# A two-block network on one core: the down product of both FFNs, from four blocks of K to one pass of eleven K pairs

## The reference, cut to what matters

```
def swiglu(x, w_gate, w_up, w_down):
    return (jax.nn.silu(x @ w_gate) * (x @ w_up)) @ w_down
f1 = swiglu(rms_norm(x, ffn1_pre_g), ...)
x = x + 0.5 * rms_norm(f1, ffn1_post_g)
m = token_mixer(rms_norm(x, mix_pre_g), ...)
x = x + rms_norm(m, mix_post_g)
f2 = swiglu(rms_norm(x, ffn2_pre_g), ...)
x = x + 0.5 * rms_norm(f2, ffn2_post_g)
```

## Time and profile before

| | us |
|---|---|
| median of 3 timed runs | 4001.05 |
| lowest and highest of them | 3992.30, 4002.52 |
| the profiled execution itself | 3995.18 |
| its span in the profile | 3993.3 |
| first down phase, 481.83 to 742.31 | 260.48 |
| second down phase, 1990.30 to 2251.30 | 261.00 |

### The profile page before, as it was taken

How to read it: one execution, slowest core, us unless ns; L and a number is a source line. 1 busy time by engine, 2 the same in 40 slices (tenths; PEclk the granted TensorE clock), 3 DMA queues, 4 the chain that set the end, 5 groups by cost and what they waited for, 6 DMA issues and landing times.

```text
span 3993.3 us, 50138 instructions
## 1 busy us (share of the span) xinstructions
PE 3769.9 (94%) x19892; PEld 3051.9 (76%) x19892; DVE 2422.4 (61%) x3232; ACT 1640.2 (41%) x2775; POOL 1788.9 (45%) x1176
## 2 busy tenths in 40 slices
PE   6999998899999899899989899999999999999998
PEld 4788776566665466788777689999968988888877
DVE  6655588744455538666578786654477436666664
ACT  4333333422222234333333443421283346666663
POOL 1555577344544452455577334332261233344364
PEclk9999999999999899999999999999999999999989
DMA  2222331110000021222331001121112310000024
GB/s 102 79 85 85 130 108 53 53 44 26 23 22 16 16 101 57 76 82 80 121 129 53 16 32 50 41 102 64 51 54 70 118 48 29 22 29 29 24 67 139
DMA packets 102218, 252.28 MB, mean 63 GB/s; under 512 B 12321, under 2 KB 15937, under 8 KB 101601
## 3 DMA queue, kind: packets, MB, share of 16 engines
q1 hardware_dynamic: 90096, 204.71, 15.2%
q0 software_dynamic: 9328, 41.75, 2.8%
q10 hardware_dynamic: 2560, 2.61, 0.2%
HBM read 200.47 MB, written 48.56 MB: 62 GB/s over the span
## 4 chain that ended last, share of the span: by engine, by line
PE 69%; DVE 17%; POOL 5%; ACT 5%; issue 3%; DMA 1%; SPq 0%; ACTq 0%; DVEq 0%; POOLq 0%
PE ps L936 6%; PE ps L937 6%; PE ps L938 6%; PE ps L418 5%; PE ps L419 5%; PE ps L420 5%; PE ps L4143 4%; PE ps L4075 2%; PE ps L4077 2%; PE ps L4076 2%; PE ps L1886 2%; PE ps L1888 2%; PE ps L1887 2%; PE ps L4127 2%; POOL fwl L820 2%
## 5 line engine op out<-in xcount | busy, mean ns | idle before, releaser
L392 POOL TENSOR_TENSOR wlo<-raw,whi 128x1024 fp32r<-128x1024 f32 x154 | 377.0, 2452 | 472.2 <-ACT whi L383 472.2
L418 PE MATMUL ps<-xh,whi 128*128 128x352 f32 (+1 forms) x1400 | 473.4, 338 | 6.1 <-DVE xl L674 2.7
L419 PE MATMUL ps<-xh,wlo 128*128 128x352 f32 (+1 forms) x1400 | 450.6, 322 | 0.0
L420 PE MATMUL ps<-xl,whi 128*128 128x352 f32 (+1 forms) x1400 | 450.0, 321 | 0.0
L820 POOL TENSOR_TENSOR fwl<-fpa,fwh 128x512 fp32r<-128x512 f32 x184 | 261.4, 1432 | 285.4 <-ACT fwh L811 283.2
L820 POOL TENSOR_TENSOR fwl<-fpb,fwh 128x512 fp32r<-128x512 f32 x180 | 258.1, 1444 | 291.1 <-ACT fwh L811 288.9
L4448 POOL TENSOR_TENSOR ospl<-osp,osph 128x672 fp32r<-128x672 f32 (+4 forms) x144 | 191.0, 1327 | 357.9 <-ACT osph L4269 356.8
L954 PE MATMUL ps<-fxh,fwh 128*128 128x512 f32 x616 | 255.5, 415 | 60.5 <-DVE acc L1167 30.3
L418 PEld LDWEIGHTS ps<-xh,whi 128*128 128x128 f32 x1400 | 265.1, 189 | 17.6 <-issue 5.7
L419 PEld LDWEIGHTS ps<-xh,wlo 128*128 128x128 f32 x1400 | 264.6, 189 | 8.0 <-issue 2.2
L1122 DVE TENSOR_TENSOR u<-ps,u 128x512 f32<-128x512 f32 x120 | 82.6, 689 | 301.0 <-PE ps L938 301.0
(11 more groups left out here) (506 smaller groups left out, 10113.7 us busy)
## 6 DMA issues: line engine op xcount, KB each, us to landing
raw<-in_w_dram SPq DMA_DIRECT2D x154, 512.0 KB, 3.7
fpa<-in_fg_dram SPq DMA_DIRECT2D x88, 256.0 KB, 3.6
fpb<-in_fg_dram SPq DMA_DIRECT2D x88, 256.0 KB, 3.4
hs_scratch<-u SPq DMA_DIRECT2D x88, 256.0 KB, 2.0
fyh<-hs_scratch SPq DMA_DIRECT2D x46, 256.0 KB, 5.9
fyl<-hs_scratch SPq DMA_DIRECT2D x42, 256.0 KB, 5.3
rs_scratch<-res POOLq DMA_DIRECT2D x2, 4160.0 KB, 14.3
frc<-in_fd_dram SPq DMA_DIRECT2D x32, 256.0 KB, 5.7
```

The source lines that it names most:

```text
L392: pool.x.tensor_tensor(K.wlo[n % 3][:, :], K.raw[n % 2][:, :], K.whi[n % 3][:, :], ALU.subtract).then_inc(*S.up("w_lo", n))
L418: pe.x.matmul(out, wh, xh, start=k == 0, stop=False)
L419: pe.x.matmul(out, wl, xh, start=False, stop=False)
L420: last = pe.x.matmul(out, wh, xl, start=False, stop=k == K - 1)
```

## The change

The blocks are gone. Each product runs over all eleven pairs before the next begins (steps ("down", m, k)), so each product is added up in PSUM and read once: 28 totals for an FFN. The bank sets are (0, 1, 2, 6) and (7, 4, 5, 3), and the order M1, M5, M6, M3, M7, M2, M4 alternates between them throughout. Sums change engines: DVE makes the weight sums (`dve_down_sum`), POOL makes the row sums, and only for M6, M7 and M4 (`pool_row_sum`). The row sum of M5 is no longer made in the down phase: the gate phase stores a third tile D for each j, the difference of its two halves (22 more stores, with one DVE subtraction each). Weights and rows stream through rings of eight tiles; D tiles of the first eleven j are kept in SBUF (`ftop`), running sums of weights in `fsum`. There are 88 weight loads and 88 row loads for an FFN. SP waits, load by load, for the user of the ring place eight loads before.

The mixed rows at the start of an FFN are split anew: POOL does 4 subtractions for M5 and 8 for M4, ACT 12 scalings, DVE 28 instructions; ACT's high parts of M4's rows, ahead of the gate steps before, now stand in the second of them, still ahead of the read of M1. Behind the first FFN, norm a (half 0, complete after M7) is squared, summed, rooted and partly applied inside the steps of M4; behind the second FFN all of the norms' work stands behind the last step, the sums of squares too.

```
-            if n == NSTEP - 1:
-                after.beside(p)
         S.steps[f, n] = "pe_step", (f, n)
+        if m == "M4":
+            after.beside(k)
...
+def dve_down_sum(dve, f, n):
+    if not FIRST_DOWN <= n < NSTEP or STEPS[n][1] not in RAW_SUMS:
+        return
+    _, m, k = STEPS[n]
+    total, at = K.fsum[k], RAW_AT[n]
+    for i in at:
+        slot_landed(dve, f, i)
+    first = raw_slot(K, at[0])
+    if m == "M5":
+        dve.wait_ge("pe_step", (f, STEP_AT["gate", 21, "M4"]))
+        out, x, y, op = total, first, raw_slot(K, at[1]), ALU.add
+    elif m == "M6":
+        dve.wait_ge("fw_lo", (f, STEP_AT["down", "M5", k]))
+        out, x, y, op = total, total, first, ALU.subtract
+    else:
+        dve.wait_ge("dve_fsum", (f, STEP_AT["down", "M6", k]))
+        out, x, y, op = first, first, total, ALU.subtract
+    dve.x.tensor_tensor(out, x, y, op).then_inc(*S.up("dve_fsum", (f, n)))
...
+def pool_row_sum(pool, f, n):
+    if not FIRST_DOWN <= n < NSTEP or STEPS[n][1] not in ("M6", "M7", "M4"):
+        return
+    at, top = ROW_AT[n], K.ftop[k]
+    for i in at:
+        row_landed(pool, f, i)
+    first = row_slot(K, at[0])
+    if m == "M7":
+        x, y = first, row_slot(K, at[1])
     else:
+        pool.wait_ge(f"ld_ft{k % 4}", (f, k))
+        x, y = (first, top) if m == "M6" else (top, first)
+    pool.x.tensor_tensor(first, x, y, ALU.subtract).then_inc(*S.up("ft_sum", (f, n)))
...
+A_BANKS, D_BANKS = (0, 1, 2, 6), (7, 4, 5, 3)
+def down_bank(m, p):
+    return (A_BANKS if m in ("M1", "M6", "M7", "M4") else D_BANKS)[p]
...
     for n in range(FIRST_GATE, NSTEP):
         pool_operand(pool, f, n + 4)
-        if FIRST_DOWN <= n + 5 < NSTEP:
-            raw_sum(pool, f, n + 5)
+        pool_row_sum(pool, f, n + 5)
...
         dve_row_low(dve, f, n + 3)
-        dve_row_sum(dve, f, n + 4)
+        dve_down_sum(dve, f, n + 5)
+        if STEPS[n][1] == "M4":
+            after.beside(STEPS[n][2])
...
+        for i, q in zip(RAW_AT[n], DOWN_RAWS[m]):
+            if i >= 8:
+                user = RAW_USER[i - 8]
+                sp.wait_ge("dve_fsum" if STEPS[user][1] in ("M5", "M6") else "fw_lo", (f, user))
+            sp.x.dma_start(raw_slot(K, i), A["fd"][f - 1, int(q), k])
...
+        for i, (c, past) in zip(ROW_AT[n], DOWN_ROWS[m]):
+            if i >= 8:
+                user = ROW_USER[i - 8]
+                if i - 8 == ROW_AT[user][0]:
+                    sp.wait_ge("ft_lo", (f, user))
+                else:
+                    sp.wait_ge("ft_sum", (f, user))
```

More of the change, by code:

```diff
@@ L460, in __init__ @@
         self.second, self.pairs = second, pairs
-        self.head = tag in ("n1", "n3")
+        self.head = not second
         if second:
@@ L713, in _ffn_steps @@
         out.extend(("gate", j, m) for m in ORDER)
-    for b, (k0, k1) in enumerate(BLOCKS):
-        for m in ORDER:
-            out.extend(("down", b, m, k) for k in range(k1 - k0))
+    for m in ORDER:
+        out.extend(("down", m, k) for k in range(KT))
     return out
@@ L751, in raw_landed, with slot_landed, row_landed @@
 def raw_landed(e, f, step, q):
[L753 to L766, removed]
+    e.wait_ge(f"ld_fr{step[1] % 2}{q}", (f, "gate", step[1], 0))
+def slot_landed(e, f, i):
+    e.wait_ge(f"ld_fr{i // 4 % 2}{i % 4}", (f, "down", i))
+def row_landed(e, f, i):
+    e.wait_ge(f"ld_fh{i % 8}", (f, i))
 def same(step, m):
-    return STEP_AT[step[:2] + (m,) + step[3:]]
+    return STEP_AT[step[:2] + (m,)]
 def raw_sum(e, f, n):
     S, K, step = e.S, e.K, STEPS[n]
-    if step[0] == "std" or step[2] not in RAW_SUMS:
+    if step[0] != "gate" or step[2] not in RAW_SUMS:
         return
@@ L806, in act_operand @@
         act.wait_ge(*S.unit_free(last - (last - n // 2) % 3))
-    if step[2] in RAW_SUMS:
-        act.wait_ge(sum_name(step), (f, n))
-    else:
-        raw_landed(act, f, step, q)
-    act.x.activation(ring(K, n)[0], raw_tile(K, step, q), ACT.Copy).then_inc(*S.up("fw_hi", (f, n)))
+    down = step[0] == "down"
+    if step[1 if down else 2] in RAW_SUMS:
+        act.wait_ge("dve_fsum", (f, n))
+    elif down:
+        slot_landed(act, f, RAW_AT[n][0])
+    else:
+        raw_landed(act, f, step, RAW_OF[step[2]])
+    raw = down_raw(K, n) if down else raw_tile(K, step, RAW_OF[step[2]])
+    act.x.activation(ring(K, n)[0], raw, ACT.Copy).then_inc(*S.up("fw_hi", (f, n)))
 def pool_operand(pool, f, n):
@@ L944, in down @@
     def down(n):
-        _, b, m, k = STEPS[n]
-        end = k == BLOCKS[b][1] - BLOCKS[b][0] - 1
+        _, m, k = STEPS[n]
+        end = k == KT - 1
         wh, wl = operand(n)
@@ L1126, in times, with difference @@
         dve.x.tensor_tensor(out, out, other, ALU.mult).then_inc(*S.up("dve_fe", (f, j, what)))
+    def difference(j, out, x, y, *need):
+        for what in need:
+            dve.wait_ge("dve_fe", (f, j) + (what if isinstance(what, tuple) else (what,)))
+        dve.x.tensor_tensor(out, x, y, ALU.subtract).then_inc(*S.up("dve_fe", (f, j, "D")))
     def beside(j, m):
@@ L1198, in dve_ffn @@
         dve_row_low(dve, f, n + 3)
-        dve_row_sum(dve, f, n + 4)
+        dve_down_sum(dve, f, n + 5)
+        if STEPS[n][1] == "M4":
+            after.beside(STEPS[n][2])
     for p in range(4):
-        total(len(BLOCKS) - 1, "M4", p)
-        if p == 1:
-            after.beside(3)
-    after.beside(5)
+        total("M4", p)
     after.end()
@@ L1264, in sp_ffn, with store @@
+    def store(j):
+        p = j % 2
+        sp.wait_ge("dve_fe", (f, j, "D"))
+        first, second, third = (1, 3, 0) if j < STD else (1, 0, 3)
+        for c, u in ((0, first), (1, second)):
+            sp.x.dma_start(A["hs"][c, j], K.u[4 * p + u][:, :]).then_inc(*S.up(f"st_h{p}{c}", (f, j), 16))
+        sp.x.dma_start(A["hs"][2, j], K.u[4 * p + third][:, :]).then_inc(*S.up(f"st_d{p}", (f, j), 16))
     if f == 2:
```

439 lines of the change are left out of this document (228 added, 211 removed).

## The result

| | before | after |
|---|---|---|
| median of the timed runs, us | 3999.27 (4 runs) | 3975.75 (3973.34 to 3980.22, 4 runs) |
| span of the profiled execution | 3993.3 | 3973.5 |
| first down phase | 481.83 to 742.31, 260.48 | 480.7 to 741.6, 260.9 |
| second down phase | 1990.30 to 2251.30, 261.00 | 1977.1 to 2224.4, 247.3 |

The account below looks back on a forecast made before the run. PE was taken as the bound, with POOL setting the down phases' pace. Savings of 42.2 + 31.5 + 17.0 + 14.5 - 4.3 = 100.9 us from 3995.2 gave 3894; 8 in 10 between 3862 and 3940, bounds 3855 to 3955.

Parts of the forecast that it names:

- first down phase: Down steps of the first FFN, with norm a moved into M4: 229.0 us forecast, saving 31.5.
- second down phase: Down steps of the second FFN: 209.3 + 7 + 2 + 0.5 = 218.8 us forecast, saving 42.2.
- starts of the FFNs: Waits before gate step M6: less mixing on DVE starts M6 near 94.6, saving 8.5 us twice, 17.0.
- behind the first FFN: Stretch after the first FFN: norm work done in M4 and no wait for a's sums, saving 14.5 us.
- behind the second FFN: Stretch after the second FFN: sums of squares of chunk a now follow the last step, costing 4.3 us.
- that link is cut: Down phase: today's chain of sum, rounding, subtraction in one iteration ends; argued against "No lead" at 3.74 us a step.
- The 7 us of operand waits: Down phase, per FFN: M6 leaves 1.9 us and M7 4.9 us that the operands' lead does not cover.
- slower: Rival, chance 0.04: weight sums queue through DVE, ACT, POOL at 4.3 us in all 44 steps; 4020 us.
- No lead: Rival, chance 0.17: waits through ACT eat the lead, M6 and M7 run at 3.74 us exposed; 3932 us.
- Norm a in M4: First down phase: five sums on PE, waits for POOL's pair and clock cost 10.2 us.
- no gain at the starts: Rival, chance 0.07: POOL's eight subtractions hold its operand 10 and DVE's sums, +17 us; 3911 us.
- the rival "clock": Rival, chance 0.06: 0.76 us waits in M6 and M7 bring half clock, 5 us lost four times; 3914 us.

Follow-up runs that it names:

- e1: Changed kernel with DVE's weight sum of step n+5 placed before its low part of the rows of n+3: 3909.64 us.
- b1: Kernel before the change, with POOL's weight sum of step n+5 placed before its operand n+4: 3966.34 us.
- e2: Changed kernel with ACT rounding the row of n+3 before the weight of n+4, from the fifth down step on: 3915.14 us.
- e5: e1 with norm a's pair of squares 4, 5 added at k = 3 and squares 4 to 7 summed together at k = 4: 3900.15 us.
- e10: e1 plus the edits of e5 and e6, and M4's eight subtractions moved back from POOL to DVE: 3886.77 us.
- e6: e1 with ACT copying the banks of M1 and M5 before operand 12 and the rounding of M4's mixed rows: 3902.88 us.

## Why the prediction was wrong

Against the profile of before, 100.9 us of gain were forecast and the span became 19.8 us shorter. The 81.1 missing are these:

| term | forecast | measured | missing |
|---|---|---|---|
| first down phase | 31.5 | -0.4 | 31.9 |
| second down phase | 42.2 | 13.7 | 28.5 |
| starts of the FFNs, with what lies up to the down phases | 17.0 | 6.8 | 10.2 |
| behind the first FFN | 14.5 | 6.8 | 7.7 |
| behind the second FFN | -4.3 | -5.1 | 0.8 |
| the rest of the kernel | 0 | -2.0 | 2.0 |

Of the 6.8 at the starts only 1.1 lie before the first down phase. The other 5.7 lie in a stretch that holds the whole mixer, and there single profiles differ by as much with no line changed: from the first down phase's end to the second FFN's first gate step it is 835.7 us in the changed kernel and 842.1 in e1.

- *The reading of before was right as far as it went.* The block starts were paid by POOL's pace; b1 shows that its sum and rounding stood in a loop. All four idle times went.
- *The step that failed: "that link is cut".* The prediction counted operations per engine and turns between DVE and POOL, and gave ACT no part in the pace, because "POOL's operand n+4 was summed an iteration earlier". It asked how early a sum stands in its own queue, five steps ahead, and not what stands ahead of it there: a low part that needs ACT, which is waiting for the sum before. The 7 us of operand waits (9.5 with clock and first wait) were 38.0 in the second phase. Being five steps ahead in the program is no lasting lead in time, when the queue in front of it is held by its own result: M5 and M3 were priced at 2.3 to 2.4 us a step, which was to keep and rebuild the lead, and the loop turned at 3.19 in both. e1 and e2 cut the loop at either end and regain some 60 and 54 us (66 and 61 as the medians stand); this is shown.
- *The size of the turns was right.* 3.48 us a step was priced, 3.40 measured, once the loop is out. The lead then covers more than was granted: 4.3 us for the phase instead of 9.5.
- *The rival "slower" had the price, 4.3 us a step, by luck.* Its chain ran from DVE's sum over ACT's rounding to POOL's subtraction (1.77 + 0.63 + 1.74 + 0.2), and POOL's subtraction is no part of the loop, which goes back to DVE over ACT's second rounding and DVE's low part. In e1 POOL's subtraction stands behind the sum as before, at 1.74 us, and the pace is 3.40. It also had the pace in all 44 steps with weight sums: it holds for some 20, and is 3.19 in M3 and, hidden from PE, in M5. It was given 0.04 on the argument that failed. "No lead" had 3.74 us a step, too little. The bound for the whole term, 22.4, came from the pace of before, which was itself that of a shorter loop; the chain of four instructions through two queues should have been the upper bound. And the bounds given for the terms, added up, reach from about 3850 to 3980, not from 3855 to 3955.
- *Norm a in M4* was priced 10.2 us; the two down phases differ by 260.9 - 247.3 = 13.6. The wait was seen and named, but 5.67 us long instead of 4; e5 takes 7.4 us off.
- *Starts of the FFNs.* M6 starts at 102.73, not 94.6. That POOL would delay what DVE gave up was the rival "no gain at the starts", and it held: DVE's four low parts of M7 took 6.9 us. M4's last sum ended as late as before, and the read of M1 is behind it. The walk through the queues was right in its links and wrong in its durations, which were those of engines alone. With M4's sums on DVE and the read moved (e10) PE has M6 at 92.68.
- *Behind the first FFN,* "the first mixer product right behind M4" was wrong: it came 11.6 us behind. PE takes the five sums of squares of b first, and they wait for POOL's pairs. The gain was 6.8 us, above the lower bound of 5. Behind the second, the first product came 16.0 us behind the end, against 10.9: 5.1 later, and DVE's reading 3.4 later, where 4.3 was forecast for both.
- *Loads and clock.* Loads were rightly put at nothing: PE and DVE wait for no load in a down phase and ACT 2.1 and 3.1 us in all; the DMA share was 0.50 and 0.53. The clock was priced at 2 us in each phase, and the granted clock was 1.00 in the second, and 0.99 in the first, where PE ran at 0.50 from 717 to 722 us, behind its wait for the pair. In 560 to 574 us PE was busy 10.22 of 14.00 us at a granted clock of 1.00, the level of 2.4 GHz, so the rival "clock" did not come. The Trainium skill, page "TensorE: Matmul & The Clock Gate", section "A second HAM failure mode: psum-queue depth-cycling", reports of another kernel that frequent short idle times made the clock oscillate. By that the clock should have done so here; the trace disagrees.

## What to carry to other kernels

Where each engine runs its own ordered program, walk one iteration round all of them: from an instruction to who waits for it, to what stands behind that one in its queue, and on, until you are back; the sum of that ring is a lower bound of the time for a step, whatever each engine's load. Make an operand before you use an older one (the sum first, the low part second), and put a read that frees a bank ahead of work that is needed later. When a phase has every engine idle for a quarter of the time, look for the ring before you move work.

## What the runs showed of the hardware

- DVE and POOL subtractions of 128x512 in float32 slow each other when both engines have one all the time: DVE 1.78 and POOL 1.74 us each, and each engine starts one every 1.70 us, against 0.68 and 1.30 us alone. A batch of four on DVE took 6.92 us beside POOL, and 3.58 with most of the overlap gone. The Trainium skill, page "GPSIMD Engine Reference", section "8. Key points", says that GpSimd shares its SBUF interfaces with VectorE and names contention with VectorE instructions that have two SBUF inputs, as these subtractions have. This case agrees, and the section gives no price.
- Idle times of 1.27 us in every 4.26 us, ten in a row, did not lower PE's clock. Longer ones do not act by their length alone: in e6 one of 8.66 us, and one of 2.60 us, were each followed by a granted clock near 0.5 (6 us and 3.4 us long), but one of 3.17 us at the same place of the second FFN by 1.00.
- Less idle time can cost more clock: in the first FFN 17.3 us in one piece had 4.4 us of half clock behind it (e1), 8.66 and 2.60 us together 9.4 us (e6).
